# Placing a sixth Strassen group in the first feed-forward of a two-block transformer kernel

## The reference

```python
def swiglu(h, w_gate, w_up, w_down):
    return (jax.nn.silu(h @ w_gate) * (h @ w_up)) @ w_down
```

## Time and profile before

| | |
|---|---|
| median of 3 runs | 1991.56 us (1989.99 to 1991.77) |
| the profiled execution's own time | 1991.87 us |
| its span, first to last instruction | 1990.1 us |
| mean granted TensorE clock in it | 0.992 |
| PE busy | 1934.5 us (97%) |
| DVE busy | 1446.9 us (73%) |
| ACT busy | 965.9 us (49%) |
| POOL busy | 144.0 us (7%) |

### The profile page before, as it was taken

The page is one execution under the profiler, slowest core; times in us unless marked ns, Lnnn a source line. Parts: engine busy times, 40 slices in busy tenths (PEclk is TensorE's granted clock), DMA queues, the critical chain, the costliest instruction groups (busy, mean ns, idle before and its releaser), DMA issues.

```text
span 1990.1 us, 30335 instructions
## 1 busy us (share of the span) xinstructions
PE 1934.5 (97%) x12001; PEld 1083.6 (54%) x12001; DVE 1446.9 (73%) x2461; ACT 965.9 (49%) x1677; POOL 144.0 (7%) x105
## 2 busy tenths in 40 slices
PE   9999999999999999999999999999989999999997
PEld 4444444445664884445444854865545544476476
DVE  6979654549987677776579758888866646966877
ACT  4448733434443344346455435455478844634442
POOL 2000000122323102000001000000000000100000
PEclk9989999999999999999999999999999999999999
DMA  7300043312332333420423241335400041424211
GB/s 246 107 1 1 22 146 106 97 54 86 116 124 74 120 116 109 127 62 14 138 60 94 104 162 54 108 105 162 170 1 1 1 127 39 126 86 148 86 64 43
DMA packets 55373, 179.44 MB, mean 90 GB/s; under 512 B 6336, under 2 KB 12096, under 8 KB 54976
## 3 DMA queue, kind: packets, MB, share of 16 engines
q1 hardware_dynamic: 55232, 177.51, 28.3%
HBM read 174.34 MB, written 2.10 MB: 89 GB/s over the span
## 4 chain that ended last, share of the span: by engine, by line
PE 87%; DVE 9%; issue 2%; ACT 2%; DMA 1%; SPq 0%; DVEq 0%; ACTq 0%
PE pS L1253 11%; PE pS L1254 11%; PE pS L1255 11%; PE pS L1319 4%; PE pS L1318 4%; PE pS L1320 4%; PE pS L1549 3%; PE pO L1584 3%; PE pS L1421 2%; PE pS L1422 2%; PE pS L1427 2%; PE pS L1514 2%; PE pT L1514 1%; DVE w_lo L2342 1%; PE pT L1253 1%
## 5 line engine op out<-in xcount | busy, mean ns | idle before, releaser
L2342 DVE SCALAR_TENSOR_TENSOR w_lo<-w_raw,w_hi 128x1024 f16<-128x1024 f32 (+2 forms) x384 | 469.1, 1234 | 77.2 <-ACT w_hi L1834 43.5
L1834 ACT ACTIVATE w_hi<-w_raw 128x1024 f16<-128x1024 f32 (+3 forms) x383 | 379.6, 1020 | 193.6 <-DVE w_raw L2362 116.8
L1253 PE MATMUL pS<-xx,w_hi 128*128 128x512 f16 x952 | 360.7, 379 | 1.7 <-DVE xx L2377 1.7
L1255 PE MATMUL pS<-xx,w_lo 128*128 128x512 f16 x952 | 360.8, 379 | 0.0
L1254 PE MATMUL pS<-xx,w_hi 128*128 128x512 f16 x952 | 360.7, 379 | 0.0
L1318 PE MATMUL pS<-arena,w_hi 128*128 128x256 f16 x705 | 192.2, 273 | 0.0
L1319 PE MATMUL pS<-arena,w_hi 128*128 128x256 f16 x705 | 192.2, 273 | 0.0
L1320 PE MATMUL pS<-arena,w_lo 128*128 128x256 f16 x705 | 192.2, 273 | 0.0
L1255 PEld LDWEIGHTS pS<-xx,w_lo 128*128 128x128 f16 x952 | 93.1, 98 | 112.5
L1253 PEld LDWEIGHTS pS<-xx,w_hi 128*128 128x128 f16 x952 | 93.2, 98 | 109.3 <-DVE xx L2377 2.5
L1254 PEld LDWEIGHTS pS<-xx,w_hi 128*128 128x128 f16 x952 | 93.1, 98 | 106.7 <-issue 0.7
(11 more groups left out here) (481 smaller groups left out, 3855.8 us busy)
## 6 DMA issues: line engine op xcount, KB each, us to landing
w_raw<-in_w SPq DMA_DIRECT2D x288, 512.0 KB, 4.2
w_raw<-in_w SPq DMA_DIRECT2D x12, 704.0 KB, 4.4
w_raw<-in_w SPq DMA_DIRECT2D x22, 256.0 KB, 3.0
X<-in_x SPq DMA_DIRECT2D x8, 264.0 KB, 7.5
arena<-in_c SPq DMA_DIRECT2D x2, 1024.0 KB, 7.2
out_t<-X SPq DMA_DIRECT2D x16, 128.0 KB, 1.7
arena<-in_h SPq DMA_DIRECT2D x4, 256.0 KB, 13.0
arena<-in_h SPq DMA_DIRECT2D x2, 512.0 KB, 11.2
```

Source lines behind the costliest of these rows:

```text
L1253: pe.matmul(ps, wh, ah, start=f, stop=False)
L1255: mm = pe.matmul(ps, wl, ah, start=False, stop=l)
L1834: act.activation(to_, from_, ACT.Copy, scale=WS).then_inc(hi_split, 1)
L2342: dve.scalar_tensor_tensor(out=lo_[:, a:], in0=from_[:, a:], scalar=WS, in1=hi_[:, a:], op0=ALU.mult, op1=ALU.subtract).then_inc(lo_split, 1)
```

## The change

Five groups at pairs 5, 8, 11, 14 and 17 become six at 4, 6, 9, 11, 14 and 16. The classic parts become pairs 0 to 3, 5, 7 and 8, 10, 12 and 13, 15, and 17 to 21. Nothing else is edited; the order of the streamed weights, the counts of semaphores and the banks follow from the same table.

```diff
@@ -74,7 +74,7 @@
 BANKS = {"qn": (3, 2, 1, 0), "ffd0": (5,), "dn0a0": (5, 3), "dn1a0": (5, 3), "dn0b0": (5,), "dn1b0": (5,)}
 CLOSED = ("ffd7", "up0a", "up1a")
-GROUPED = (5, 8, 11, 14, 17)
+GROUPED = (4, 6, 9, 11, 14, 16)
```

## The result

The changed kernel takes 1998.28 us (median of 6 runs, 1997.93 to 1998.79); the kernel before, run beside it, 1991.13 us (6 runs, 1987.28 to 1991.77). It is slower by 7.15 us between the medians, where +8.6 was forecast. The ratio of the means is 1.0040, 95% interval 1.0027 to 1.0053. The profiled execution took 1998.17 us with a span of 1996.4 us, against 1991.87 and 1990.1.

What follows compares the result with a forecast made beforehand. PE, busy 97% of the span, was taken to bound the kernel. The terms -1.19 + 7.8 - 1.15 + 2.3 + 0 + 0 + 0.8 = +8.6 us on 1991.56 gave 2000.2 us, range 1995.5 to 2004 us.

Steps and rivals of the forecast that it cites:

- The saving: In the feed-forward, one classic pair becomes a group, 9.17 us of PE instead of 10.36: -1.19 us.
- The first group's wait for bank 0: Group 4's first product waits on PE until DVE evicts pair 3's first tile: +7.8 us, bounds 7.0 to 8.2.
- the two shorter splits: Ahead of that eviction in DVE's queue, two weight units split 4 tiles instead of 8: -1.08 us.
- the third sum: DVE's third sum (line 2358), formerly right behind pair 3's first eviction, now comes before it: +0.7 us.
- POOL's sum: POOL adds group 6's weights right behind its first mix, slowing DVE beside it: +0.7 us, bounds 0 to 0.9.
- The old stall inside the first group: PE's waits in the first group, the longest for a weight split of DVE, go away: -1.15 us.
- The clock: PE's idle gap ahead of group 4 drops the granted clock to half: +2.3 us, bounds 0 and 3.4.
- Groups 6, 11 and 16: Groups one classic pair behind another wait for bank 0: 0, 0 and +0.8 us, together bounded by 0 and 2.5.
- rival 4: Single pairs never let DVE recover; groups 6, 11, 16 stall 1 to 2 us each: up to 2004 us; chance 0.10.
- Rival 1: PE stalls ahead of the first group but the clock holds: 1996.3 to 1999.2 us; chance 0.15.
- rival 3: Group 4's first product is not held because bank 0 is free: 1989.2 to 1990.4 us; chance 0.07.
- rival 2: The first group's stall is much smaller, since DVE lags less: 1993.5 to 1995.5 us; chance 0.08.

Runs made afterwards that it cites:

- experiment 5: Changed kernel with pair 3's two tiles in banks 2 and 3 instead of 0 and 1; stage 206.05 us, whole 1997.85 us (one run).
- experiment 9: Changed kernel with DVE's two splits of the mixed input cut from 1024 to 64 columns, only to time DVE; whole 1996.56 us (one run).
- experiment 1: Changed kernel with five groups at 4, 8, 11, 14, 17 instead of its six; stage 205.44 us, whole 1997.48 us, ratio 1.0046 to the kernel before.
- experiment 7: Changed kernel with POOL's sum for group 6 behind its second mix instead of its first; stage 205.93 us, whole 1998.88 us (one run).
- experiment 10: Changed kernel with the last group at 17 instead of 16; stage 205.55 us, whole 1999.73 us (one run).
- experiment 6: Changed kernel with 32 matmuls whose result nobody reads ahead of the first group, keeping PE busy in the gap; whole 1996.64 us (one run).
- experiment 3: Changed kernel with seven groups at 5, 7, 9, 11, 13, 15, 17 instead of its six; stage 203.46 us, whole 1992.51 us (one run).
- experiment 4: Changed kernel with its six groups at 6, 8, 10, 12, 14, 16; stage 203.82 us, whole 1995.90 us (one run).
- experiment 8: Changed kernel with its six groups at 6, 9, 11, 13, 15, 17; stage 198.07 us, whole 1991.15 us, ratio 1.0005 to the kernel before.
- experiment 2: Changed kernel with its six groups one pair later, at 5, 7, 10, 12, 15, 17; stage 201.59 us, whole 1990.92 us (one run).

## Why the prediction was right

*The saving*, -1.19 us. It is there: pairs of 10.36 us and groups of 9.17 us follow each other, but stalls take it back wherever two groups stand close.

*The first group's wait for bank 0*, +7.8 us, measured +7.67 (15.97 to 23.64 us behind the norm). The place is shown by experiment 5 and by the eviction that ends 0.1 us ahead of PE's start; the cause, DVE's backlog since the norm, by experiment 9, one for one. Of its parts, read from start to start in DVE's queue, the two shorter splits gave -0.88 and not -1.08; the third sum +0.95, of which 0.34 came back because the first sum of S2 no longer stood beside POOL's mix, so +0.61 and not +0.7; POOL's sum +0.47 and not +0.7 (experiments 1 and 7). Three errors of 0.1 to 0.2 us nearly cancel.

*The old stall inside the first group*, -1.15. Group 4 takes 10.47 us, 1.35 of it for the clock, so 9.12 against a group's 9.17: the stall is gone.

*The clock*, +2.3, measured +1.35, half of 2.70 us. The fall came as forecast and the size was the term most off, within its bounds; the sign named for it, 3 to 7 us at 0.50 behind the gap, was missed with 2.70. In five kernels with the gap it cost 1.35, 1.8, 2.2, 2.6 and 2.6 us, as PE's return fell at another point of the half-clock stretch. The last is experiment 10, the same code up to there, so 2.3 lies between two values of one program: how near it comes in a given run is luck. That its price and group 6's wait are not to be added was half right: without the fall group 6 waited 0.5 us (experiment 6), where 1.3 was forecast. By the Trainium skill, TensorE: Matmul & The Clock Gate, section "Why this matters for your kernels", an idle gap between bursts of matmuls puts the clock back if it is long enough. The trace agrees for the five gaps here with PE idle for 5.6 to 7.5 us; which shorter ones do it, the runs leave open (last section).

*Groups 6, 11 and 16*: 0, 0 and +0.8, measured 0.05, 0 and 0.84. The numbers came out, the reason given for them only in part. From group 9's start the eviction ended at 18.8 us (18.6 forecast), from group 14's at 20.3 (20.3). But parity decides only while DVE has a lead from two classic pairs. In a row of single pairs POOL's mix falls beside the odd groups too, a group and a pair take 20.65 us against PE's 19.53, and both parities stall (experiments 3, 4 and 8). The part of rival 4 that said so is right as a mechanism; the change, with two pairs after each single one, just does not show it.

*The sum*, by these measured terms: -1.19 + 7.67 - 1.15 + 1.35 + 0.05 + 0.84 = +7.57 us, against +7.51 in the stage. The two profiled executions differ by 6.30 us, the stage's 7.51 less what was won ahead of it (0.08) and behind it; the medians of six runs differ by 7.15. The forecast's +8.6 was too high mainly by the clock, and by what was won behind the stage, which no term of it covered.

Rival 1 (the clock holds) and rival 3 (no wait) are refuted by the trace, and rival 2 by a stall of 7.67 us where it needed less than 6. Its own numbers don't fit each other: a net under 4 us leaves 5.5 us for the stall and the clock together, and an eviction at 460.4 is 5.9 us of stall alone. What stays open: why the stalls of experiment 4, 0.5 to 2.4 us, are so unequal, and whether the backlog could be worked off sooner by giving DVE's splits of the mixed input to another engine, or the bank freed sooner by writing pair 3's gate eviction further ahead in DVE's order. Neither was tried.

## What to carry to other kernels

Where an engine that empties the banks is held up by a norm while PE runs on, the reserve is counted in banks: look up who writes the next bank and when its last output was read out, before moving denser work to that place. A stall there costs its length, and if the clock falls, up to half of PE's work at half clock behind it; part of that can lie under a later wait. And compare the engines over the pattern that is to be repeated, with what other engines do beside it: here a group and one classic pair are 19.53 us of PE but 20.65 us on DVE once POOL's work lies beside them. The first place and the spacing of the groups weighed more than their number: five groups took 205.44 us in the stage with the first at 4 and 196.50 with the first at 6.

## What the runs showed of the hardware

The same gap of PE ahead of the second block's first matmuls (idle 2.65 us before, 2.66 after; from start to start 3.03 and 3.04) was followed by half clock before and not after. Busy time by stretch, changed kernel:

```profile
752.40:755.55 3.15, 0.59 (x3) 0.10 (x1) 2.83 (x6) 0.68 (x2) 0.00 (x0) 1.00 0.81 252
755.55:758.95 3.40, 3.30 (x16) 1.54 (x17) 3.33 (x7) 2.98 (x7) 0.00 (x0) 1.00 1.00 384
```

Nor does the length of a gap decide it in the feed-forward. Group 7's gap was idle for 2.44 us in experiment 2 and for 2.45 us in experiment 3, in the same place; the clock fell in the first and held in the second. It fell after 2.19 us of idle time in experiment 4 and after 2.87 in experiment 5, and held after 2.74 in experiment 5 (ahead of pair 3's gate). In experiments 2, 4 and 5 it fell only when PE had been back at work for 0.27, 1.1 and 0.95 us. All five gaps of 5.6 us and more ahead of the first group had the clock at 0.50 from within the gap on.

A shift of the program in time can thus add or take such falls in code that was not touched. Behind the stage the changed kernel's lag on the one before went from 7.44 us (at 748 us) to 5.85 (at 1395), since the fall above was missing; to 7.08 (at 1452), where the clock stood at 1.00 in both and PE waited for DVE once for 1.31 us instead of 0.23, for a cause not followed up; to 4.6 (at 1603), since only the kernel before had the clock at 0.50, from 1458.1 to 1464.9; and to 6.3 at the end, after a fall that only the changed kernel had, from 1615.1 to 1618.5. The 1.14 us won back is the sum of these four. Such falls also go with much of the spread of a kernel's runs: in experiment 8 the fastest run, 1987.58 us, had a mean granted clock of 0.997 and the slowest, 1994.12 us, one of 0.991. Differences of a microsecond or so are better compared by stage than by the whole, and even in a stage only with the clock beside them.
